# First output projection with seven block products instead of eight, in two passes over the weights' rows

## What is computed

```python
def even_mixer(...):
    ...
    out = jnp.concatenate([a_out, b_out], axis=-1) @ w_out    # (tokens, 2048) @ (2048, 1024)
    return out, s_ret_new, s5_re_new, s5_im_new

def trunk(...):
    for layer in range(DEPTH):
        h = rms_norm(x, norm_w[layer])
        ...
        x = x + mix
```

## Time and profile before

| | us |
|---|---|
| median of 3 runs | 3284.24 |
| lowest, highest | 3282.04, 3288.19 |
| span of the profiled execution, first to last instruction | 3286.6 |
| of it `combine`, from its first load to the next stage's first load | 399.45 |
| of it weights and the first two tiles | 63.10 |
| of it tiles 2 to 15 and the sample tokens | 328.82 |
| of it end of the last matmul to the next stage | 7.53 |

### The profile page before, as it was taken

How to read it: one execution, slowest core, us unless ns; L and a number is a source line. 1 busy time by engine, 2 the same in 40 slices (tenths; PEclk the granted TensorE clock), 3 DMA queues, 4 the chain that set the end, 5 groups by cost and what they waited for, 6 DMA issues and landing times. The chain is left out here.

```text
span 3286.6 us, 45918 instructions
## 1 busy us (share of the span) xinstructions
PE 3094.7 (94%) x16972; PEld 2711.6 (83%) x16972; DVE 1500.8 (46%) x2880; ACT 1046.8 (32%) x1751; POOL 1078.8 (33%) x672
## 2 busy tenths in 40 slices
PE   7999899799999789897899989999999999997999
PEld 6999899688888589684688859999988888886886
DVE  7999344305430188874422212133345444445442
ACT  4111122312211155551311110024454443456741
POOL 2222222122222255560122102344434433345531
PEclk9999999899999889997899989999999989997899
DMA  5433655355542356653533222343333333333333
GB/s 138 102 123 125 199 160 178 103 133 154 171 142 92 135 194 203 209 169 118 218 128 125 105 98 86 97 152 102 116 122 130 101 131 103 126 110 124 136 118 111
DMA packets 376188, 442.86 MB, mean 135 GB/s; under 512 B 46264, under 2 KB 315192, under 8 KB 366832
## 3 DMA queue, kind: packets, MB, share of 16 engines
...
...
## 5 line engine op out<-in xcount | busy, mean ns | idle before, releaser
L796 PE MATMUL p_psum<-p_h_hi,p_w_hi 128*128 128x344 f32 (+1 forms) x1600 | 568.2, 355 | 0.0
L796 PE MATMUL p_psum<-p_h_hi,p_w_lo 128*128 128x344 f32 (+1 forms) x1600 | 562.2, 351 | 0.0
L796 PE MATMUL p_psum<-p_h_lo,p_w_hi 128*128 128x344 f32 (+1 forms) x1600 | 560.9, 351 | 0.0
L2483 PE MATMUL p_psum<-p_h_hi,p_w_hi 128*128 128x344 f32 (+1 forms) x1280 | 464.0, 362 | 8.4 <-DVE p_h_lo L2220 3.4
L2483 PE MATMUL p_psum<-p_h_lo,p_w_hi 128*128 128x344 f32 (+1 forms) x1280 | 456.5, 357 | 0.0
L2483 PE MATMUL p_psum<-p_h_hi,p_w_lo 128*128 128x344 f32 (+1 forms) x1280 | 456.4, 357 | 0.0
L380 POOL CAST p_w_hi<-p_w_raw 128x1024 fp32r<-128x1024 f32 x80 | 90.2, 1128 | 814.8 <-PE p_psum L796 671.3
L796 PEld LDWEIGHTS p_psum<-p_h_hi,p_w_hi 128*128 128x128 f32 x1600 | 302.9, 189 | 36.5 <-issue 9.3
L796 PEld LDWEIGHTS p_psum<-p_h_hi,p_w_lo 128*128 128x128 f32 x1600 | 302.8, 189 | 29.1
L796 PEld LDWEIGHTS p_psum<-p_h_lo,p_w_hi 128*128 128x128 f32 x1600 | 302.8, 189 | 28.5
L2238 DVE COPY p_out<-p_psum 128x344 f32<-128x344 f32 (+1 forms) x160 | 93.5, 586 | 482.3 <-PE p_psum L2483 482.2
...
## 6 DMA issues: line engine op xcount, KB each, us to landing
p_w_raw<-in_w_in SPq DMA_DIRECT2D x144, 512.0 KB, 4.9
z<-p_out ACTq DMA_DIRECT2D x64, 512.0 KB, 3.5
z<-p_out SPq DMA_DIRECT2D x64, 512.0 KB, 3.2
...
u_s<-p_out SPq DMA_DIRECT2D x128, 73.0 KB, 2.9
...
```

The costliest lines, as they stand in the source:

```text
L796: ins = pe.matmul(bank, wv[par][:, k, :], h[:, k, c0:c0 + n], start=(k == 0 and j == 0), stop=(k == KD - 1 and j == 2))
L2483: ins = pe.matmul(bank, wv[par][:, k, :], h[:, k, c0:c0 + n], start=(k == 0 and j == 0), stop=(k == KD - 1 and j == 2))
```

## The change

`combine` now takes two passes over the 2048 features: pass 0 uses rows 0 to 1023 of the weights, pass 1 rows 1024 to 2047. Within a pass two token tiles make a pair q (8 pairs for each pass, q = 0 to 7 and 8 to 15). The pair's tokens and the pass's features are cut in 2 x 2 blocks A11, A12 (first tile, first and second 512 features), A21, A22 (second tile); the weights of the pass in 2 x 2 blocks B11, B12, B21, B22 of 512 x 512. The 2 x 2 block product is computed by the Winograd form of Strassen's scheme:

- sums of tokens: S1 = A21 + A22, S2 = S1 - A11, S3 = A11 - A21, S4 = A12 - S2
- sums of weights: T1 = B12 - B11, T2 = B22 - T1, T3 = B22 - B12, and B21 - T2, which the code calls T4
- seven products: A11 B11, S2 T2, S3 T3, S1 T1 (the group ALPHA), A12 B21, A22 T4, S4 B22 (BETA)
- sums of products, out of PSUM and in SBUF, give the four output blocks.

A product is 12 matmuls with 512 columns (4 feature blocks, three parts) into one PSUM bank; the eight banks are used in turn. The list `products` fixes one order, by place p = 0 to 111, 56 for each pass; all engines run through it. At the start of a pass the first eight products (ALPHA of two pairs) are done jointly, a weight block k at a time (`joint`), as the weights get ready. The tokens' parts lie in a ring of ten products (`mc_hi`, `mc_lo`), prepared ten places ahead.

Who does what. GpSimd: S3, S4, the sums of weights (three additions for each k of `alpha`, two for each k of `beta`), and three additions of u for each pair (`add_u`: a partial sum `us` that goes into three output quarters). VectorE: S1, S2, all low parts of tokens (`low`) and weights (`weight`), the additions out of PSUM (`evict`), the norm. ScalarE: all high parts, a copy of the product A11 B11 to `us` (`keep_p1`), stores, squares. The output is added in place into `xo`, which is loaded with x (pass 0) or with the x1 that pass 0 has stored (pass 1); the normed result overwrites it once x1 is stored. The eight sample tokens get plain products, 40 matmuls in each pass, before place 42 of the pass. The weights of ALPHA of pass 1 are prepared at places 49 to 52 of pass 0; those of BETA at place 0 of each pass, ahead of the first `evict`.

Matmuls of the stage: 112 x 12 + 80 = 1424. The loops are unrolled now.

```diff
+def combine(nc, tag, mix, w_out, x_in, x_out, norm_w):
...
+    A11, S2, S3, S1, A12, A22, S4 = range(7)
+    B11, T2, T3, T1, B21, T4, B22 = range(7)
+    ALPHA, BETA = (A11, S2, S3, S1), (A12, A22, S4)
+    H4, PASSES, RING, N_RAW = KD // 2, 2, 10, 5
+    PAIRS = NT // 2
+    N_Q = PASSES * PAIRS
+    products = []
+    for h in range(PASSES):
+        q0 = h * PAIRS
+        for q in (q0, q0 + 1):
+            products += [(q, c) for c in ALPHA]
+        for q in (q0, q0 + 1):
+            products += [(q, c) for c in BETA]
+        for q in range(q0 + 2, q0 + PAIRS - 2):
+            products += [(q, c) for c in ALPHA + BETA]
+        for group in (ALPHA, BETA):
+            for q in (q0 + PAIRS - 2, q0 + PAIRS - 1):
+                products += [(q, c) for c in group]
+    place = {qc: p for p, qc in enumerate(products)}
+    N_P = len(products)
+    PASS = N_P // PASSES
+    JOINT = 2 * len(ALPHA)
...
-        wo_hi = sb("wo_hi", [P, n_k, D], F32R)
-        wo_lo = sb("wo_lo", [P, n_k, D], F32R)
-        m_raw = [sb(f"m_raw{i}", [P, n_k, P]) for i in range(2)]
-        m_hi = [sb(f"m_hi{i}", [P, n_k, P], F32R) for i in range(2)]
-        m_lo = [sb(f"m_lo{i}", [P, n_k, P], F32R) for i in range(2)]
+        wc_hi, wc_lo = sb("wc_hi", [P, 7, H4, BLK], F32R), sb("wc_lo", [P, 7, H4, BLK], F32R)
+        w_raw, tt = sb("w_raw", [P, N_RAW, BLK]), sb("tt", [P, 2, BLK])
+        m_raw = [sb(f"m_raw{i}", [P, 2, KD, P]) for i in range(2)]
+        mc_hi, mc_lo = sb("mc_hi", [P, RING, H4, P], F32R), sb("mc_lo", [P, RING, H4, P], F32R)
+        s3, us = sb("s3", [P, H4, P]), sb("us", [P, BLK])
+        xo = [sb(f"xo{i}", [P, 2, D]) for i in range(2)]
...
-        psum = ctx.enter_context(nc.psum_tensor(f"{tag}_psum", [P, 2, 2, BLK], F32))
+        psum = ctx.enter_context(nc.psum_tensor(f"{tag}_psum", [P, 8, BLK], F32))
...
+            def load_mixed(q):
+                h, p = q // PAIRS, q % PAIRS
+                if q >= 2:
+                    sp.wait_ge(m_lo_done, place[q - 2, S4] + 1)
+                for e in range(2):
+                    sp.dma_start(m_raw[q % 2][:, e, :, :], mix["z"][2 * p + e, :, KD * h:KD * (h + 1), :])\
+                        .then_inc(m_ld[q % 2], 16)
+            def load_x(q):
+                h, p = q // PAIRS, q % PAIRS
+                if q >= PAIRS + 2:
+                    sp.wait_ge(n_st[q % 2], 32 * ((q - PAIRS) // 2))
+                elif q >= 2:
+                    sp.wait_ge(x_st[q % 2], 32 * (q // 2))
+                src = (x_in, x_out)[h]["x"]
+                sp.dma_start(xo[q % 2][:], src[2 * p:2 * p + 2, :, :].rearrange("t p d -> p t d"))\
+                    .then_inc(x_ld[q % 2], 16)
...
+            load_mixed(0)
+            load_alpha(0, 0)
+            load_mixed(1)
+            for k in range(1, H4):
+                load_alpha(0, k)
+            load_x(0)
+            load_x(1)
...
+            for h in range(PASSES):
+                q0 = h * PAIRS
+                for k in range(H4):
+                    load_beta(h, k)
+                load_mixed(q0 + 2)
+                for q in range(q0, q0 + PAIRS):
+                    if q == q0 + 2:
+                        sp.wait_ge(w_lo_done, 28 * (h + 1))
+                        sp.wait_ge(wadd_done, 20 * (h + 1))
+                        sp.dma_start(xs, (x_in, x_out)[h]["s"]).then_inc(xs_ld, 16)
+                    if q + 3 < N_Q and q != PAIRS - 1:
+                        load_mixed(q + 3)
+                    if q == PAIRS - 2:
+                        sp.wait_ge(xs_st, 16)
+                        for k in range(H4):
+                            load_alpha(1, k)
+                    if q + 2 < N_Q:
+                        load_x(q + 2)
...
+            def alpha(h, k):
+                t = tt[:, k % 2, :]
+                b22, b12, b11 = (raw(alpha_piece(h, k, i)) for i in range(3))
+                for i in range(2):
+                    pool.wait_ge(w_ld[alpha_piece(h, k, i) % N_RAW], w_landed(alpha_piece(h, k, i)))
+                if k >= 2:
+                    pool.wait_ge(w_lo_done, w_no(h, k - 2, T2) + 1)
+                elif h:
+                    pool.wait_ge(w_lo_done, w_no(h - 1, k + 2, T4) + 1)
+                pool.tensor_tensor(t, b22, b12, ALU.subtract).then_inc(wadd_done, 1)
+                pool.wait_ge(w_ld[alpha_piece(h, k, 2) % N_RAW], w_landed(alpha_piece(h, k, 2)))
+                pool.tensor_tensor(b12, b12, b11, ALU.subtract).then_inc(wadd_done, 1)
+                pool.wait_ge(w_lo_done, w_no(h, k, T3) + 1)
+                pool.tensor_tensor(t, t, b11, ALU.add).then_inc(wadd_done, 1)
...
+                pool.tensor_tensor(t, raw(n), wc_hi[:, T2, k, :].bitcast(F32), ALU.subtract).then_inc(wadd_done, 1)
+                pool.wait_ge(wadd_done, wadd_no(h, k, 0, True) + 1)
+                pool.tensor_tensor(t, t, wc_lo[:, T2, k, :].bitcast(F32), ALU.subtract).then_inc(wadd_done, 1)
+            def add_u(q):
+                for c, e, half in ((S2, 0, 1), (S3, 1, 0), (S3, 1, 1)):
+                    pool.wait_ge(ev_done, ev_end[place[q, c]])
+                    v = quarter(q, e, half)
+                    pool.tensor_tensor(v, v, us[:], ALU.add).then_inc(v_done, 1)
...
+                    pool.tensor_tensor(s3[:], m[:, 0, 0:H4, :], m[:, 1, 0:H4, :], ALU.subtract).then_inc(s3_done, 1)
...
+                    pool.tensor_tensor(m[:, 0, H4:KD, :], m[:, 0, H4:KD, :], m[:, 0, 0:H4, :], ALU.subtract)\
+                        .then_inc(s4_done, 1)
...
+            def keep_p1(q):
+                act.wait_ge(prod_done, place[q, A11] + 1)
+                act.wait_ge(v_done, 3 * q)
+                act.activation(us[:], bank(q, A11), ACT.Copy).then_inc(s1_done, 1)
+            def store(q):
+                h, p = q // PAIRS, q % PAIRS
+                act.wait_ge(ev_done, ev_end[place[q, S4]])
+                for e in range(2):
+                    act.dma_start(x_out["x"][2 * p + e, :, :], xo[q % 2][:, e, :]).then_inc(x_st[q % 2], 16)
...
+            def low(c):
+                q, s = products[c]
+                m = m_raw[q % 2]
+                if s == A11:
+                    dve.wait_ge(s3_done, q + 1)
+                    dve.tensor_tensor(m[:, 1, 0:H4, :], m[:, 1, 0:H4, :], m[:, 1, H4:KD, :], ALU.add).then_inc(s12_done, 1)
+                dve.wait_ge(m_hi_done, c + 1)
+                dve.tensor_tensor(mc_lo[:, c % RING, :, :], raw_of(q, s), mc_hi[:, c % RING, :, :].bitcast(F32),
+                                  ALU.subtract).then_inc(m_lo_done, 1)
+                if s == A11:
+                    dve.wait_ge(s12_done, 2 * q + 1)
+                    dve.wait_ge(m_lo_done, c + 1)
+                    dve.tensor_tensor(m[:, 0, 0:H4, :], m[:, 1, 0:H4, :], m[:, 0, 0:H4, :], ALU.subtract)\
+                        .then_inc(s12_done, 1)
+            def weight(h, k, b, src):
+                dve.wait_ge(w_hi_done, w_no(h, k, b) + 1)
+                dve.tensor_tensor(wc_lo[:, b, k, :], src, wc_hi[:, b, k, :].bitcast(F32), ALU.subtract)\
+                    .then_inc(w_lo_done, 1)
...
+                if c in (S2, S3):
+                    if c == S2:
+                        dve.wait_ge(s1_done, q + 1)
+                    else:
+                        dve.wait_ge(v_done, 3 * q + 1)
+                        dve.wait_ge(ev_done, ev_end[place[q, S2]])
+                    dve.tensor_tensor(us[:], bank(q, c), us[:], ALU.add).then_inc(ev_done, 1)
+                elif c == S1:
+                    dve.wait_ge(v_done, 3 * q + 1)
+                    into(0, 1)
+                    dve.wait_ge(v_done, 3 * q + 3)
+                    into(1, 1)
...
+                dve.wait_ge(x_st[q % 2], 32 * (q // 2 + 1))
+                dve.wait_ge(const_ld, 16)
+                for e in range(2):
+                    x = xo[q % 2][:, e, :]
+                    dve.scalar_tensor_tensor(out=x, in0=x, scalar=st[:, e, 2:3], in1=wrow[:], op0=ALU.mult,
+                                             op1=ALU.mult).then_inc(y_done, 1)
...
+            for p, (q, c) in enumerate(products):
+                h, at = p // PASS, p % PASS
+                if at == 0:
+                    for k in range(H4):
+                        beta(h, k)
+                    sample_low(h)
+                evict(q, c)
+                if p + RING < N_P:
+                    low(p + RING)
+                if h == 0 and at - LAST - JOINT + 1 in range(H4):
+                    alpha(1, at - LAST - JOINT + 1)
+                if h and at - 3 >= 0 and products[p - 3][1] == S4:
+                    norm(products[p - 3][0])
...
+            def part(q, c, k):
+                p = place[q, c]
+                for j, (m, w) in enumerate(((mc_hi, wc_hi), (mc_hi, wc_lo), (mc_lo, wc_hi))):
+                    ins = pe.matmul(bank(q, c), m[:, p % RING, k, :], w[:, c, k, :],
+                                    start=(k == 0 and j == 0), stop=(k == H4 - 1 and j == 2))
+                if k == H4 - 1:
```

(27 more changed lines are left out.)

477 lines of the change are left out of this document (331 added, 146 removed).

## The result

The changed kernel takes 3315.38 us (median of 4, 3312.24 to 3318.40), the kernel before on the same chip 3286.22 (median of 4). The ratio is 1.0087, 95% interval 1.0075 to 1.0099: slower by 29 us (25 to 33). The forecast was 3298.5 in a range of 3262 to 3317. The profiled execution has a span of 3311.5 us; before had 3286.6. The stage `combine` went from 399.45 to 435.81 us (first load 1559.29, next stage's first load 1995.10), where the sum said 413.7.

The account below looks back on a forecast made before the run. TensorE was taken to bound the kernel before; the 47.2 us saved would be outweighed by 21 at the start, 29 at the border, 4 in pass 1 and 7.5 at the end: +14.3, so 3298.5 us, range 3262 to 3317.

Parts of the forecast that it names:

- the sum: Stage `combine`: 322.8 us of matmuls plus losses of 43.3, 28.6, 4 and 15 give 413.7 us against 399.45.
- TensorE's floor: Matmuls of the stage: 1424 at 0.2267 us each take at least 322.8 us.
- The start: Pass 0 up to the ninth product: it starts at 62.7 us, VectorE and GpSimd alternating; loss 43.3 us.
- With no exclusion GpSimd's chain alone gives about 45: Lower bound for the ninth product of pass 0: about 45 us instead of 62.7 if VectorE and GpSimd overlap.
- The border: Between the passes: late BETA weights let place 64 start at 64.3 us after place 49; loss 28.6 us with slow clock.
- The end: After the last matmul: last addition, squares, stores, two norms and barrier take 15 us, against 7.53 before.
- Pass 1: Steady work with the norm: VectorE needs 18 to 20.5 us a pair against TensorE's 19.0; loss 4 us, bounds 0 and 15.
- Rival C: Pass 1: VectorE with the norm becomes the bound at 21.6 us a pair, losing 15 us instead of 4; 3310 us; chance 0.17.
- Rival A: Whole stage: VectorE and GpSimd overlap more than assumed; at the extreme, stage 369 us, kernel 3254 us; chance 0.22.
- the exclusion: VectorE with two SBUF inputs and GpSimd do not run at once; their times add up, stretching operations by about 1.2 us.
- The total: Whole kernel: the stage's +14.3 us put on the median of 3284.24 give 3298.5 us.
- The other figure for a matmul: Skill page's 131 ns a matmul against the trace's 226.7: saving 27.2 us instead of 47.2, time 20 us higher.

Follow-up runs that it names:

- e8: Changed kernel with GpSimd's additions on VectorE, a third `xo` buffer with ring of 8, BETA pieces of pass 1 loaded early, squares later: 3273.8 us, ratio 0.9952 to before.
- e5: Changed kernel with each GpSimd addition of the stage replaced by three writes of about its length that read nothing, sums left out: 3296.5 us.
- e1: Changed kernel with each GpSimd addition of the stage replaced by one short write of zeros to the same columns, sums left out: 3259.7 us.
- e6: Changed kernel with all 120 GpSimd additions of the stage moved to VectorE, nothing left out: 3288.2 us, ratio 1.0001 to the kernel before.
- e7: Changed kernel with a third `xo` buffer and the ring of converted operands cut from 10 products to 8: 3299.1 us, ratio 1.0027 to the kernel before.
- e9: Changed kernel with only the ring of converted operands cut from 10 products to 8, two `xo` buffers kept: 3313.9 us, ratio 1.0069 to the kernel before.

## Why the prediction was right, and where it wasn't

- **TensorE's floor**, 322.8 us, holds. 1424 matmuls were issued, and in e8 616 of them took 140.2 us of busy time at full clock, 0.2276 each.
- **The start** was right in size: the ninth product at 60.9 us against 62.7, TensorE idle 11.8 ahead of it (some 15 forecast), released by VectorE's first addition. "With no exclusion GpSimd's chain alone gives about 45" was some 5 us too low: without holds e5, with 1.48 us for each addition, starts it at 51.8 and e1, with 0.53, at 44.9, so 1.25 us would give about 50 (an estimate on a straight line between the two).
- **The border** was right in place and size: the pieces in several short waits at places 56 to 63 (13.1 us in three, 18 forecast), then 13.0 (9 forecast), BETA's pieces behind the store of pair 7. From the end of place 49, at about 1745.2, to place 64 are 68.1 us, against 64.3. Start and border together lose 70.9 us until place 64 starts; the sum had 71.9, of which 2.4 are the slow matmuls behind it, so 69.5.
- **The end** took 14.5 and 15.8 us in the two traces (15 forecast).
- **Pass 1 is the term that was mis-sized**: 27.7 us (26.3 again), where the forecast had 4 and 2.4 for the slow matmuls behind place 64; even without these it lies outside the bounds of 0 and 15. It is 21 of the 22 us by which the stage missed its sum. The step was "Stores and the reload of `xo` (5.0 + 4.8 us) lie in the same circle. I take 4 us of loss over the pass". I had compared VectorE's 18 to 20.5 us of work a pair with 19.0, as if the work could be spread over the pair. With two buffers it can't: the additions of a pair, GpSimd's among them, the norm, the stores, squares and copy, or the reload, and the next addition wait for each other, and the circle takes 21.8 us although VectorE is busy 109 of 168. What makes it too long is the length of GpSimd's additions and the holds: in e1, with the same two buffers, ring and orders, the norms are 18.4 us apart and pass 1 loses 4.1, most of it the slow matmuls behind place 64. e5 and e6 show that the holds are about half of the loss (15.0 and 14.5 left without them), e7 and e9 that buffer and ring remove nearly all of it even with the holds.
- **Rival C came true in its sign.** The sign of being wrong, "if TensorE waits for VectorE in every pair of pass 1 (C)", is what the trace shows from place 78 on (two of the seven waits, 8.0 us, stand without a releaser), with C's period (21.8 us, 21.6 said). C had a chance of 0.17, and its price of 15 us was too low as well: the waits are 17.5 us, and slower matmuls came on top.
- **Rival A's price was wrong**, though it did not come about. "If the exclusion hardly counted" was to give 369 us. e5, without any hold, has 410.1, and GpSimd unheld at 1.25 us would lie between e5 (1.48) and e1 (0.53, 373.5), at about 401 by a straight line, an estimate. The 1.27 us of an addition, in a chain of which each link waits for the one before, is a cost of its own; I had it as hidden.
- **The total** came out 16.9 us above the forecast where the stage was 22.1 above its sum. The difference is in the time outside the stage and in the median of before, 2 us higher in this comparison. The range held, by 1.6 us, and by luck: its upper end, 3317, allows a stage of 432.2, and the stage took 435.8. That some 7 us of it did not reach the end was no part of the prediction.
- **The other figure for a matmul**, which the prediction named and which would have put the time 20 us higher, near the measured one, is not the reason: matmuls in an undisturbed stretch still stand 0.2276 us apart, so the saving of 47 us was there and was lost in waits.
